# Routing weights of one of three dense token groups: indirect accumulating DMAs into zeroed memory in place of one-hot matmuls

## The reference, cut to what matters

```python
v1, i1 = lax.top_k(s1, 16);  v2, i2 = lax.top_k(s2, 16)      # per token and head: 128 keys each
cand = v1[..., :, None] + v2[..., None, :]
best, pos = lax.top_k(cand, 16)
eidx = i1 * 128 + i2, taken at pos                            # 8 heads x 16 = 128 experts per token
g = softmax(best)
a = einsum('chkd,cd->chk', u_tab[eidx], xc)
y = einsum('chk,chkd->cd', gelu(a) * g, v_tab[eidx])
```

## Time and profile before

| | |
|---|---|
| runs of before | 2671.74 us median of 3 (2670.98 to 2674.82) |
| the profiled execution | 2670.72 us, span 2668.9 us, granted clock 0.965 of full |
| TensorE matmul busy | 2436.3 us, 91% |
| VectorE busy | 1723.6 us, 65% |
| ScalarE busy | 979.3 us, 37% |
| GpSimd busy | 403.4 us, 15% |
| HBM read, written | 533.10 MB, 70.78 MB |

### The profile page before, as it was taken

The page is one execution under the profiler, slowest core; times in us unless marked ns, Lnnn a source line. Parts: engine busy times, 40 slices in busy tenths (PEclk is TensorE's granted clock), DMA queues, the critical chain, the costliest instruction groups (busy, mean ns, idle before and its releaser), DMA issues.

```text
span 2668.9 us, 30930 instructions
## 1 busy us (share of the span) xinstructions
PE 2436.3 (91%) x12205; PEld 1866.8 (70%) x12205; DVE 1723.6 (65%) x2984; ACT 979.3 (37%) x1250; POOL 403.4 (15%) x299
## 2 busy tenths in 40 slices
PE   6998999578877899899989999989999999999997
PEld 4665786333333344677768999989999888777775
DVE  4634344421126656566544988899998578888886
ACT  4544432121103211576233343336555333333332
POOL 0100000000010000000000011132442234544430
PEclk9999999789988999999999999999999999999998
DMA  4544342699990000201032466769998799999992
GB/s 199 212 189 159 127 158 73 243 422 425 424 378 32 32 32 18 109 33 64 32 126 93 161 236 221 257 235 353 343 342 336 283 374 377 382 380 381 380 369 93
DMA packets 159277, 605.94 MB, mean 227 GB/s; under 512 B 13623, under 2 KB 79351, under 8 KB 126488
## 3 DMA queue, kind: packets, MB, share of 16 engines
q1 hardware_dynamic: 91168, 384.32, 38.3%
q0 software_dynamic: 42480, 154.68, 15.5%
q10 hardware_dynamic: 25480, 64.92, 6.2%
HBM read 533.10 MB, written 70.78 MB: 226 GB/s over the span
## 4 chain that ended last, share of the span: by engine, by line
PE 51%; DVE 22%; issue 11%; DMA 10%; ACT 4%; POOL 1%; ACTq 0%; DVEq 0%; SPq 0%; POOLq 0%
DVE window L597 6%; PE P L2599 4%; PE P L2601 4%; PE P L2600 4%; DVE part L597 4%; PE P L2254 3%; PE P L2430 3%; DVE ug L1397 3%; DMA H<-in_w_up 3%; DMA vg<-in_v,sparse 2%; PE P L2050 2%; PE P L2051 2%; PE P L2052 2%; DMA ug<-in_v,sparse 2%; DVE tmp L605 2%
## 5 line engine op out<-in xcount | busy, mean ns | idle before, releaser
L597 DVE TENSOR_TENSOR part<-raw,part 128x2048 fp32r<-128x2048 f32 x136 | 311.2, 2289 | 167.4 <-ACT part L1903 165.6
L2599 PE MATMUL P<-hr,part 128*128 128x384 f32 (+1 forms) x1136 | 398.6, 351 | 17.2 <-DVE part L597 16.5
L2600 PE MATMUL P<-hr,part 128*128 128x384 f32 (+1 forms) x1136 | 392.7, 346 | 0.0
L2601 PE MATMUL P<-hr,part 128*128 128x384 f32 (+1 forms) x1136 | 392.7, 346 | 0.0
L2718 POOL DMA_INDIRECT ug<-in_ur,sparse x128 | 176.9, 1382 | 1208.6 <-DVE window L1289 744.7
L2703 PE MATMUL P<-part,ge 128*128 128x512 f32 x768 | 301.8, 393 | 11.0 <-DVE part L597 10.3
L2704 PE MATMUL P<-part,ge 128*128 128x512 f32 x768 | 299.0, 389 | 0.0
L2705 PE MATMUL P<-part,ge 128*128 128x512 f32 x768 | 299.0, 389 | 0.0
L1903 ACT ACTIVATE part<-raw 128x2048 fp32r<-128x2048 f32 x136 | 260.5, 1915 | 101.1 <-PE P L2705 81.8
L2599 PEld LDWEIGHTS P<-hr,part 128*128 128x128 f32 x1136 | 215.5, 190 | 28.2 <-DVE part L597 22.2
L2600 PEld LDWEIGHTS P<-hr,part 128*128 128x128 f32 x1136 | 215.5, 190 | 5.0
(11 more groups left out here) (359 smaller groups left out, 4362.6 us busy)
## 6 DMA issues: line engine op xcount, KB each, us to landing
raw<-in_u SPq DMA_DIRECT2D x64, 1024.0 KB
raw<-in_vd SPq DMA_DIRECT2D x64, 1024.0 KB
W<-in_w_up SPq DMA_DIRECT2D x24, 2048.0 KB, 20.2
W<-in_w_in SPq DMA_DIRECT2D x18, 2048.0 KB, 7.8
W<-in_ada_w SPq DMA_DIRECT2D x12, 2048.0 KB, 7.7
a_scratch<-gt ACTq DMA_DIRECT2D x128, 192.0 KB
w_scratch<-window ACTq DMA_DIRECT2D x12, 2048.0 KB, 12.1
wr<-w_scratch SPq DMA_DIRECT2D x32, 768.0 KB, 13.1
```

Of the source, the lines that this page charges most:

```text
L597: return v.tensor_tensor(out=out_, in0=in0, in1=in1, op=op)
L2599: t.matmul(b, wh[:, k, js], HR[0][:, k, lo:S], start=k == 0, stop=False)
L2600: t.matmul(b, wh[:, k, js], HR[1][:, k, lo:S], start=False, stop=False)
L2601: ins = t.matmul(b, wl[:, k, js], HR[0][:, k, lo:S], start=False, stop=k == 7)
```

## The change

Only groups 2 and 3 go through the one-hot steps: x runs from 16 to 47, and the transposes and spreads of group 1 are gone. For group 1 VectorE computes 128 offsets per token into `Wd[0:4]` (OFS) and keeps the shares (WGT), both [128 tokens, 128 columns]; GpSimd then issues 128 indirect DMAs, one per column, each of which adds 128 single float32 values to HBM. The 16 columns of a head hold different experts and may be in flight together; before the next head's, GpSimd waits until all earlier ones have landed (`wa`). `Wd[0:4]` (8.4 MB) is filled with zeros by four GpSimd DMAs after the first block's attention. ScalarE's loads of the rotary tables wait for that fill, since the zeros lie where a table will. The readers of `Wd` wait for all 128 adds. Cut to its core:

```diff
+        OFS, WGT = TOK32[:, 1920:2048].bitcast(u32), TOK32[:, 0:128]
...
-        wg_steps = interleave([("wg", x, i) for x in range(48) for i in range(2)], dots, 0.75) + dots
+        wg_steps = interleave([("wg", x, i) for x in range(16, 48) for i in range(2)], dots, 0.75) + dots
...
+        POOL_STEPS, adds, ready = [("row", k) for k in range(3)], [("add", k) for k in range(128)], False
+        for kind, *i in ORDER3:
+            ready = ready or (kind, i) == ("gt", [1])
+            if kind == "ud":
+                POOL_STEPS.append(("row", i[0] + 3))
+                for _ in range(1 + i[0] % 2):
+                    if ready and adds:
+                        POOL_STEPS.append(adds.pop(0))
+        POOL_STEPS += adds
...
 (VectorE, columns)
+                elif q == 1:
+                    tk_inc(stt(num, hk2(I1), 32.0, par("slot").broadcast_to([128, 128]), MUL, ADD))
+                    tk_inc(stt(num, hk2(I2), 4096.0, num, MUL, ADD))
+                    tk_inc(v.tensor_copy(OFS, num), "ofs")
...
 (GpSimd, once TensorE is done with the attention)
+            gp.wait_ge(s["att_mm"], 68)
+            g.memset(zeros, 0.0).then_inc(s["z_v"], 1)
+            gp.wait_ge(s["z_v"], 5)
+            for b in range(4):
+                nc.gpsimd.dma_start(Wd[b].rearrange("p (r n) -> p r n", n=S), zeros.unsqueeze(1).broadcast_to([128, 8, S])).then_inc(s["wz"], 16)
...
+            def add_weights(k):
+                gp.wait_ge(s["wz"], 64)
+                gp.wait_ge(s["tk_v"], mark["ofs"])
+                gp.wait_ge(s["wa"], 256 * (k // 16))
+                g.indirect_dma_start(out=Wd[0:4].rearrange("b p (x o) -> (b p x) o", o=1), out_offset=bass.IndirectOffsetOnAxis(ap=OFS[:, k:k + 1], axis=0),
+                                     in_=WGT[:, k:k + 1], in_offset=None, compute_op=ADD).then_inc(s["wa"], 16)
...
-                    a.dma_start(Wd[tb], WS[tb % 2]).then_inc(s[f"ws{tb % 2}"], 16)
+                    a.dma_start(Wd[tb + 4], WS[tb % 2]).then_inc(s[f"ws{tb % 2}"], 16)
...
 (readers of Wd and of the window's memory: ScalarE "up", GpSimd rows of v, SyncE "spill")
-                    act.wait_ge(s["ws0"], 96)
-                    act.wait_ge(s["ws1"], 96)
-                    act.wait_ge(s["wg_mm"], 96)
+                    act.wait_ge(s["ws0"], 64)
+                    act.wait_ge(s["ws1"], 64)
+                    act.wait_ge(s["wg_mm"], 64)
+                    act.wait_ge(s["wa"], 2048)
```

More of the change, by code:

```diff
@@ L17 @@
                   ("g2", 8), ("gf2", 8), ("gfin", 8), ("qg2", 1), ("kg2", 1), ("hcw", 36), ("hcb", 12),
-                  ("hb1", 1), ("hb2", 1), ("hb3", 1), ("hfr", 1), ("cc", 16), ("half", 32), ("odd", 32), ("row0", 16)]:
+                  ("hb1", 1), ("hb2", 1), ("hb3", 1), ("hfr", 1), ("cc", 16), ("half", 32), ("odd", 32), ("row0", 16), ("slot", 1)]:
     PCOLS[_name] = (_n, _n + _w)
@@ L1364, in shares @@
                 tk_wait()
-                dst = GW if q else GW0.rearrange("p (h k) -> p h k", h=8)
+                dst = GW if q > 1 else (WGT if q else GW0).rearrange("p (h k) -> p h k", h=8)
                 tk_inc(tt(dst, GW, GR.unsqueeze(2).broadcast_to([128, 8, 16]), MUL), ("it", q))
@@ L1375, in columns @@
                     tk_inc(v.tensor_copy(EID, num), "eid")
-                    mark["tx", 0] = tk[0]
+                elif q == 1:
+                    num = EQ[:, 0:1, 0:8, :].rearrange("p h k j -> p (h k j)")
+                    tk_wait()
+                    tk_inc(stt(num, hk2(I1), 32.0, par("slot").broadcast_to([128, 128]), MUL, ADD))
+                    tk_wait()
+                    tk_inc(stt(num, hk2(I2), 4096.0, num, MUL, ADD))
+                    tk_wait()
+                    tk_inc(v.tensor_copy(OFS, num), "ofs")
+                    mark["tx", 1] = tk[0]
                 else:
@@ L2765, in row_of_v @@
                     if k % 8 < 4:
-                        gp.wait_ge(s["wg_v"], 241)
-                        gp.wait_ge(s["wg_mm"], 96)
+                        gp.wait_ge(s["wg_v"], 161)
+                        gp.wait_ge(s["wg_mm"], 64)
+                        gp.wait_ge(s["wa"], 2048)
                     rows(VG[(k + 4) % 8], A["v"], EID[:, k:k + 1], s[f"vg{k % 4}"])
-            for kind, *i in ORDER3 + V_STEPS:
+            for kind, k in POOL_STEPS:
+                if kind == "row":
+                    row_of_u(k)
+                else:
+                    add_weights(k)
+            for kind, *i in V_STEPS:
                 if kind == "ud":
-                    for k in range(4) if i[0] == 0 else (i[0] + 3,):
-                        row_of_u(k)
+                    row_of_u(i[0] + 3)
                 elif kind in ("vr", "sw"):
@@ L2875, in sync_program @@
                 elif kind == "spill":
-                    sp.wait_ge(s["ws0"], 96)
-                    sp.wait_ge(s["ws1"], 96)
-                    sp.wait_ge(s["wg_v"], 241)
-                    sp.wait_ge(s["wg_mm"], 96)
+                    sp.wait_ge(s["ws0"], 64)
+                    sp.wait_ge(s["ws1"], 64)
+                    sp.wait_ge(s["wg_v"], 161)
+                    sp.wait_ge(s["wg_mm"], 64)
+                    sp.wait_ge(s["wa"], 2048)
                     chunk(0)
```

66 lines of the change are left out of this document (34 added, 32 removed).

## The result

| | before | after |
|---|---|---|
| median of 4 runs | 2673.01 us (2670.98 to 2674.82) | 2741.38 us (2738.32 to 2745.41) |
| ratio | | 1.0254, 95% interval [1.0242, 1.0266] |
| first fx matmul, first matmul of the last stage | 1364.3, 2103.4 us | 1372.4, 2173.6 us |
| the stretch between the two | 739.1 us | 801.2 us |

The change costs 68 us where I had predicted a gain of 17 to 18. In the two profiles the stretch from the first fx step to the last stage is 62 us longer, and it starts 8 us later. Most of these 8 us arise in the stage of the first block's experts. What of the 8 us is the change's, no run tells, and I leave them out of the account.

What follows compares the result with a forecast made beforehand. VectorE was taken as the limit before, with TensorE just behind and deciding afterwards. The terms -39 (removed work) + 6 (DMA engines) + 13 (tail) + 3 (waits) gave -17 us, forecast 2654 us, range 2628 to 2696.

Steps and rivals of the forecast that it cites:

- What bounds before: From first one-hot step to last fx step: VectorE decides, 11.6 us per two fx steps, TensorE just behind at 11.3.
- the gain of the removed work: One-hot to last fx stretch: dropping 16 of 48 steps makes TensorE the limit, 325 to 286 us, gaining 39.
- The tail term: Behind the last one-hot step, 20 crowded dots wait on DMA: 13 us lost, range 3 to 30.
- Small edits and zero fill at nothing: Before 1778 us: offsets gain at most 1 us, merged semaphores cost nothing, the zero fill hides after the first attention.
- the issue on GpSimd: One-hot part: 1.2 us per add, so a gather and 1.5 adds take 3.0 of 4.5 us per dot and fit.
- rival 2: GpSimd is the bound: adds at 3 us make 5.7 us per dot against 4.5, about 2715 us; chance 0.05.
- D: The experiments' theory that the adds' single floats take time on the DMA engines.
- The waits for landings: GpSimd's wait for all earlier adds, once in 16: 2 to 14 us each, 3 us altogether, range 0 to 20.
- Time on the DMA engines: One-hot part: 56 ns per added float makes 11.0 us per two fx steps against TensorE's 10.7, costing 6 us (0 to 30).
- Rival 1: Single floats fill the DMA engines at 112 ns per element: 23 us slower, 2694 us; chance 0.25.
- VectorE at 90%: Sign expected in the changed profile: VectorE busy about 90% in the one-hot part if the prediction is about right.
- Wrong altogether: Failure sign: the stretch to the last fx step not between 286 and 325 us.

Runs made afterwards that it cites:

- no_adds_even: Changed kernel with all 128 adds left out and the 67 dots dealt evenly over the 64 half steps; 2642.02 us, ratio 0.9886.
- no_adds: Changed kernel with all 128 adds and the wait for them left out, zero fill kept; 2660.35 us, ratio 0.9946.
- fill_only: Kernel before the change plus the zero fill of Wd[0:4] alone, all 48 one-hot steps kept; 2672.27 us, ratio 1.0003.
- run 2741: The changed kernel itself, all 128 adds in place, against the kernel before; median 2741.38 us, ratio 1.0254.
- pool_only: Changed kernel with every add replaced by eight GpSimd memsets, 2.06 us in all, without DMA; 2706.88 us, ratio 1.0131.
- half_gaps: Changed kernel with 64 of group 1's tokens by 64 two-column adds, 40 one-hot steps, dots even, adds paused before each wait; 2674.63 us, ratio 1.0008.
- half_no_adds: Changed kernel with 40 one-hot steps, 64 of group 1's tokens meant for adds, but those 64 adds left out; 2655.51 us, ratio 0.9946.
- pool_long: Changed kernel with every add replaced by ten GpSimd memsets, 2.6 us in all, without DMA; 2747.10 us, ratio 1.0273.
- plain_scatter: Changed kernel with the 128 adds made plain scatters of the same floats to the same places, without accumulating; 2695.67 us, ratio 1.0079.

## Why the prediction was wrong, step by step

**What bounds before, and the gain of the removed work: right.** I said that TensorE takes over from VectorE, with 39 us to gain and some of it lost in a crowded tail. `no_adds_even` gains 31 us, with TensorE at 272.80 of 276. The tail term was too small: `no_adds` gains 12, so 27 of the 39 are gone where I had 13 and less without the adds (the crowding itself, by the pair of runs, is 18). I had also let 49 us of DMA decide the tail and passed over GpSimd's 40, already more than TensorE's 34; with the measured prices its 18 adds and 16 gathers take 67.

**Small edits and zero fill at nothing: right** (`fill_only`, 1.0003).

**The step that failed is the issue on GpSimd: "I take 1.2", and from it "3.0 us of it" and "so it fits".** An add took 1.97 us as a mean and 2.27 of the queue. The step went wrong in three places, which add up:

- The nearest row was a gather with the same 128 indices, and I took its median. The accumulating form has a price of its own: 1.55 us at least, 1.60 median. Its mean under load is 1.97, as the gather's was 1.48 in this stage against a median of 1.15. A queue is filled by means.
- I left out the 0.30 us between DMA instructions. In before it hardly shows, as nearly all gathers waited for a dot and the gap hid in that wait; but it is there, as "<-issue 0.3" for one gather in the earlier trace rows and 14 times (4.3 us) from 1600 to 2180. With it an add takes 2.27 us of the queue, a gather 1.61.
- A dot therefore asks GpSimd for 1.61 + 1.5 x 2.27 = 5.0 us where TensorE gives it 4.5; with the 22.6 us of waits over 85 dots (128 adds at 1.5 per dot) it is 5.3. I had 3.0.

With the gap counted, the point from which GpSimd decides isn't the 2.2 us of my rival 2 but (4.5 - 1.61)/1.5 - 0.30 = 1.6 us, and 1.45 with the waits. The shortest add in the trace lasts 1.55. My own upper bound of 3.06 said that it "would not" fit, and I gave that case 0.05.

**Rival 2 is what happened,** by the first sign I had named for it (GpSimd "without gaps": 274.8 of 276 us are taken). The second, "adds of over 2 us", holds only with the gap, 2.27. It had 2715, though its terms, -39 + 58 + 30, give 2721; the run 2741. Its price can be checked by the other runs: the adds take 128 x 2.27 + 22.6 = 313 us of GpSimd, 49 more than the 264 of `pool_only`. At 0.58 per us that is 28 us above its 47, 75 of the 81 us that the adds cost. The remaining 6 are within what this way of reckoning can tell, and are about what is left for D here.

**The waits for landings, "3 us for all waits together, 0 to 20": too small.** They are 22.6 us on GpSimd, 3.2 each, and by the slopes above about 14 us of the run (an estimate). The single wait lies where I had put it (2 to 14 us; the seven take 1.9 to 6.1). The slack of the four row buffers that was to hide it was gone, since GpSimd itself was late.

**Time on the DMA engines, 56 ns per float: high, and not what decided.** Queue rows from 1778 to 2054 (packets, MB, share of 16 engines), of after, of `half_gaps` and of `half_no_adds`:

```profile
q0 software_dynamic: 18955, 27.84, 39.1%
```
```profile
q0 software_dynamic: 16816, 37.66, 42.6%
```
```profile
q0 software_dynamic: 10080, 36.70, 36.9%
```

16 x 276 = 4416 engine-us. Without adds 0.369 x 4416/36.70 = 44.4 engine-us per MB. After: 0.391 x 4416 - 27.84 x 44.4 = 491 us for 80 adds, 48 ns per float. `half_gaps`: 209 us for 48 adds, 34 ns. These are upper ends: in the runs without adds a MB has more engine time where fewer rows move, 48.8 us in `pool_long`, and with that after gives 36 ns. The single packets of q0 in the trace say the same directly: in after 10073 packets of 4 bytes, one per float, last 36 ns as a mean, 366 engine-us or 8% of the window; in `half_gaps` 31 ns. (Each DMA, gather or add, leaves 16 more of 4 bytes that last 9 ns; they are not counted.) Rival 1 needed 112. The share of the engines in after was 0.85, below before's 0.90. I had spent most of the working and a quarter of the chances on the resource that got idler.

**The signs.** I wanted VectorE at 90%: it was at 76. "The last stage equally long" and "the stage of the zero fill unchanged" held. "Wrong altogether" was to be a stretch outside 286 to 325 us from the first one-hot step to the last fx step. From the first one-hot matmul to the last fx matmul it went from 321 us (1781.3 to 2102.3) to 376 (1796.7 to 2172.5).

## What to carry to other kernels

Before work is given to an engine that looks idle, ask what it feeds: GpSimd was busy 15% of the span, and its gathers still set the pace of VectorE and TensorE once each had 1.5 adds queued in front. Sum the queue time of every instruction for one turn of the loop, with mean durations under load, the gap between two DMA instructions, and the waits; on an engine that mostly waits for something else the gap hides in those waits, and the few instructions that did not wait show it. If one bound of the sum lies below the turn and the other above it, as here 3.0 and 5.7 us around 4.5, the chance of that limit isn't small.

## What the runs showed of the hardware

- **An accumulating indirect DMA takes 0.6 us longer to issue** than a plain one with the same indices and data (median 1604 against 1006 ns, least 1552 against 958), and a gather of 128 rows of 4 KB takes about as long as a plain scatter of 128 floats (932 ns at least): between these two the size of an element doesn't enter. The Trainium skill, "DMA: Bandwidth & Descriptors", Anatomy of one DMA, puts most of the fixed 2 us of a DMA on the landing and calls descriptor generation "small, variable". These runs show it as anything but small for the queue: an instruction holds GpSimd for 1.0 us (plain) to 1.6 us (accumulating) as a median, and here that was most of the loss. Those 2 us are a latency; the issue is an occupancy.
- **0.30 us lie between two DMA instructions of GpSimd,** 120 times before the adds (36.6 us in all). Behind memsets the gap is 0.15.
- **Plain scattered floats travel together, accumulated ones alone.** From 1778 to 2054 us these are the packets of after and, in the second line, of `plain_scatter`:

```profile
DMA packets 28977, 73.82 MB, mean 267 GB/s; under 512 B 13280, under 2 KB 18532, under 8 KB 25316
DMA packets 22471, 80.94 MB, mean 293 GB/s; under 512 B 5044, under 2 KB 10932, under 8 KB 18551
```

The single packets of q0 tell why. A plain scatter of 128 floats leaves 16 packets of 32 bytes, 14 ns each (1435 of them for the 90 issued here); an accumulating one leaves 128 packets of 4 bytes, 36 ns each (10073 for 80); the 16 of 9 ns come with both. That is 0.2 against 4.6 us of engine time per DMA. The Trainium skill, "DMA: Bandwidth & Descriptors", Specifications, expects a read-modify-write below 512 B. In the plain form no price of that kind can be seen in the 14 ns.

- **The granted clock is lower in the windows in which TensorE waits more**: 0.94 from 1778 to 2054 us and 0.77 from 2054 to 2104, with TensorE busy 236.49 of 276 and 25.78 of 50 us, against 0.99 and 1.00 before. These are means of stretches at 1.2 and at 2.4 GHz. `pool_only` shows 0.93 with no add at all, so the adds are not needed for it. How much of the slope is the clock, no run separates.
